# Weight units fetched two to a transfer, in runs of 8 KB a partition, on three double buffers

## The reference, cut to what matters

```python
def reference(x, ...):
    x = first_block(x, ...)    # S5 scan + banded attention + gates, w_out, then PEER
    return second_block(x, ...) # modulation by c, NSA attention + short conv, w_out, then PEER

def peer(xn, w_query, sub_keys, u_tab, v_tab):   # in both blocks; 8 heads, 16 experts a head
    q = xn @ w_query                             # (512, 1024)
    # scores against 2 x 128 sub keys a head, top 16 of each, top 16 of their 256 sums
    # -> 128 expert numbers and 128 gates for each token
    a = einsum('cd,ced->ce', xb, u_tab[eb])      # 128 rows of u for each token
    w = gb * gelu(a)
    return einsum('ce,ced->cd', w, v_tab[eb])    # 128 rows of v for each token
```

## Time and profile before

| | before |
|---|---|
| median of 3 runs | 3286.17 us (3284.38 to 3288.89) |
| the profiled execution's own time | 3282.93 us |
| its span in the trace | 3281.1 us |
| granted TensorE clock | 0.85 |
| bytes read from HBM | 1289.62 MB, 394 GB/s over the span |
| busy: TensorE, VectorE, ScalarE, GpSimd | 75%, 71%, 41%, 34% |

### The profile page before, as it was taken

One profiled execution on the slowest core, in us unless ns is written; L12 is line 12 of the kernel. 1 busy time (PEld: TensorE's weight loads), 2 busy tenths in 40 slices (PEclk: granted clock), 3 DMA queues, 4 the chain that ended last, 5 costly groups with the idle time before them and its releaser, 6 DMA issues.

```text
span 3281.1 us, 40578 instructions
## 1 busy us (share of the span) xinstructions
PE 2445.8 (75%) x14052; PEld 1029.2 (31%) x14052; DVE 2320.1 (71%) x5500; ACT 1330.7 (41%) x3602; POOL 1129.2 (34%) x1038
## 2 busy tenths in 40 slices
PE   8868779776797777979787869878887655554555
PEld 3442333223332233335342426423334211111111
DVE  7439694778839787385875685987866777777644
ACT  2114432444424444243583343467734433333322
POOL 0012342324413243243343333443433444443432
PEclk9979889987898988989888979878888877778777
DMA  9899999999999999999999999999999999999997
GB/s 247 304 351 415 399 410 386 411 397 414 413 389 416 415 411 412 371 397 401 383 379 388 397 402 399 406 419 410 378 411 400 413 420 420 419 418 409 420 420 318
DMA packets 214057, 1295.01 MB, mean 395 GB/s; under 512 B 26934, under 2 KB 30294, under 8 KB 82776
## 3 DMA queue, kind: packets, MB, share of 16 engines
q0 software_dynamic: 148320, 1076.50, 80.9%
q1 hardware_dynamic: 64860, 213.81, 17.2%
q10 hardware_dynamic: 672, 2.12, 0.2%
HBM read 1289.62 MB, written 2.71 MB: 394 GB/s over the span
## 4 chain that ended last, share of the span: by engine, by line
PE 35%; DMA 25%; DVE 22%; issue 8%; ACT 4%; POOL 3%; SPq 0%; POOLq 0%; DVEq 0%; ACTq 0%
PE ps L1722 12%; DMA ring<-in_k_uv,idx 10%; DMA ring<-in_k_vu,idx 9%; PE ps L1802 9%; DVE ring L415 9%; DMA wsl<-in_k_wu 6%; PE ps L2096 6%; POOL ring L2400 3%; DVE big L470 2%; PE ps L2106 2%; ACT L1249 2%; PE ps L1779 1%; PE ps L1977 1%; DMA wsl<-in_k_wmod 1%; ACT diag L1249 1%
## 5 line engine op out<-in xcount | busy, mean ns | idle before, releaser
L1722 PE MATMUL ps<-ring,diag 64*64 64x512 f32 x8192 | 1255.7, 738 | 483.1 <-ACT diag L1249 459.1
L415 DVE CUSTOM_DVE_ANT_0 ring<-ring,xn 128x1024 f32<-128x1024 f32 x1024 | 1238.8, 1220 | 440.9 <-DMA ring<-in_k_vu,idx 231.7
L2400 POOL DMA_INDIRECT ring<-in_k_vu,idx x514 | 559.5, 1089 | 1136.7 <-DVE aw L415 645.6
L2400 POOL DMA_INDIRECT ring<-in_k_uv,idx x510 | 563.6, 1105 | 940.1 <-DVE aw L415 643.2
L1722 PEld LDWEIGHTS ps<-ring,diag 64*64 64x64 f32 x8192 | 308.2, 157 | 1240.0 <-ACT diag L1249 733.2
L1249 ACT ACTIVATE aw<-aw 128x2 f32<-128x2 f32 x512 | 103.7, 202 | 1008.8 <-DVE aw L415 1007.3
L1802 PE MATMUL ps<-wsl,xT 128*128 128x512 f32 x896 | 427.6, 623 | 36.5 <-DMA wsl<-in_k_wu 32.3
L1249 ACT ACT_TABLE_LOAD x339 | 434.9, 1283 | 22.8 <-issue 10.7
L1249 ACT ACTIVATE diag<-gid,aw 128x64 f32<-128x64 f32 x1024 | 312.0, 342 | 315.1 <-PE ps L1722 298.9
L1249 ACT ACTIVATE gid<-ident,gate 128x64 f32<-128x64 f32 x1024 | 292.4, 332 | 0.0
L1802 PEld LDWEIGHTS ps<-wsl,xT 128*128 128x128 f32 x896 | 167.0, 196 | 296.0 <-issue 226.4
(11 more groups left out here) (264 smaller groups left out, 2112.1 us busy)
## 6 DMA issues: line engine op xcount, KB each, us to landing
wsl<-in_k_wu SPq DMA_DIRECT2D x342, 512.0 KB, 8.8
wsl<-in_k_wmod SPq DMA_DIRECT2D x40, 512.0 KB, 6.4
ring<-in_k_vu,idx POOLq DMA_INDIRECT x514
ring<-in_k_uv,idx POOLq DMA_INDIRECT x510
ring<-in_k_wmod SPq DMA_DIRECT2D x8, 512.0 KB, 10.5
wsl<-in_k_wu SPq DMA_DIRECT2D x8, 280.0 KB, 26.4
hres<-in_x SPq DMA_DIRECT2D x4, 512.0 KB, 6.0
pers<-L1d POOLq DMA_DIRECT2D x8, 256.0 KB, 13.0
```

Of the source, the lines that this page charges most:

```text
L415: V(v.tensor_tensor_reduce(u_row(s), u_row(s), xn[:, n % 3, :], 1.0, 0.0, ALU.mult, ALU.add, aw[:, b, k:k + 1]), ("dot", s))
L1722: r = t.matmul(PA[half][64 * q:64 * q + 64, :], diag[64 * half:64 * half + 64, s % (2 * PAIR), :], v_row(s)[64 * half:64 * half + 64, 512 ...
L2400: Q(p.indirect_dma_start(out=both_rows(s), out_offset=None, in_=tab, in_offset=bass.IndirectOffsetOnAxis(ap=idx[:, n % 2, k:k + 1], axis=0 ...
```

## The change

The list of units is turned into `order`, in which an empty place follows each unit of `sk`, so that every pair of places (0 and 1, 2 and 3, ...) is two units of the same matrix and tile, or `sk` and nothing. `two_units(k)` takes the place of `unit(k)`: it waits for the use of both units that were in the pair of buffers, and issues one transfer for both (1 MB; 512 KB for `sk`). The host lays the two units of a pair side by side for each partition, so that a partition's part is one run of 8 KB; in the units of 280 columns the SBUF side stays in pieces. The eight early units become four transfers in the same manner. What TensorE waits for and marks stays one unit at a time: both marks of a pair stand on the one transfer. `extra(k)` is called ahead of each pair; all its places are at the first unit of one. The products and their order are the same.

```diff
-        early = [carve(rflat, at + 1024 * e, 2, 512)[0] for at in (2048, 11264) for e in range(4)]
+        early2 = [carve(rflat, at + 2048 * e, 4, 512)[0] for at in (2048, 11264) for e in range(2)]
+        early = [w[:, 2 * e:2 * e + 2, :] for w in early2 for e in range(2)]
...
-        unit_at = {(n, name, b, u): k for k, (n, name, b, u, *_) in enumerate(units)}
+        order = [w for u in units for w in ([u, None] if u[1] == "sk" else [u])]
+        unit_at = {w[0:4]: k for k, w in enumerate(order) if w}
+        assert all(x[0:3] == y[0:3] for x, y in zip(order[0::2], order[1::2]) if y)
...
-            def unit(k):
-                n, name, b, u, nk, key, c0, nn, at = units[k]
-                if k >= NWS:
-                    Y.wait_ge("unit_used", k - NWS)
+            def two_units(k):
+                n, name, b, u, nk, key, c0, nn, at = order[k]
+                count = 2 if order[k + 1] else 1
+                for j in range(k, k + count):
+                    if j >= NWS and order[j - NWS]:
+                        Y.wait_ge("unit_used", j - NWS)
                 src = A["k_wmod" if name == "mod" else "k_wu%d" % (n // 4)]
-                src = src[at:at + 256 * nn].rearrange("(p k n) -> p k n", p=128, n=nn)
-                Q(s.dma_start(wsl[:, k % NWS, :, 0:nn], src), "w%d" % (k % NWS), ("unit", k))
+                src = src[at:at + 256 * nn * count].rearrange("(p k n) -> p k n", p=128, n=nn)
+                dst = wsl[:, k % NWS:k % NWS + count, :, :].rearrange("p j k n -> p (j k) n")[:, :, 0:nn]
+                Q(s.dma_start(dst, src), "w%d" % (k % NWS), *[("unit", k + j) for j in range(count)])
...
-                    for e, w in enumerate(early):
-                        src = A["k_wmod"][131072 * e:131072 * e + 131072].rearrange("(p k n) -> p k n", p=128, n=512)
-                        Q(s.dma_start(w, src), "early%d" % e, ("early", e))
+                    for e, w in enumerate(early2):
+                        src = A["k_wmod"][262144 * e:262144 * e + 262144].rearrange("(p k n) -> p k n", p=128, n=512)
+                        Q(s.dma_start(w, src), "early%d" % e, ("early", 2 * e), ("early", 2 * e + 1))
...
-            unit(0)
-            unit(1)
+            two_units(0)
             load(craw[:, :, :], A["k_s5c"], "craw")
-            for k in range(2, NWS):
-                unit(k)
+            for k in range(2, NWS, 2):
+                two_units(k)
...
-            for k in range(NWS, len(units)):
+            for k in range(NWS, len(order), 2):
                 extra(k)
-                unit(k)
+                two_units(k)
...
-        arr["k_wu%d" % layer] = np.concatenate(laid)
-    arr["k_wmod"] = I["w_mod_2"][0].reshape(4, 2, 128, 12, 512).transpose(3, 0, 2, 1, 4).reshape(-1)
+        both = [np.stack([x.reshape(128, -1) for x in laid[k:k + 2]], 1).reshape(-1) for k in range(0, len(laid), 2)]
+        arr["k_wu%d" % layer] = np.concatenate(both)
+    arr["k_wmod"] = I["w_mod_2"][0].reshape(2, 2, 2, 128, 12, 512).transpose(4, 0, 3, 1, 2, 5).reshape(-1)
```

More of the change, by code:

```diff
@@ L2426, in extra @@
             def extra(k):
-                n, name, b, u = units[k][0:4]
+                n, name, b, u = order[k][0:4]
                 if (n, name, b, u) == (0, "attb", 0, 0):
```

## The result

| | before | after |
|---|---|---|
| median | 3285.28 us (6 runs, 3276.84 to 3288.89) | 3298.41 us (6 runs, 3294.60 to 3301.26) |
| ratio | | 1.0049, 95% interval 1.0034 to 1.0064 |
| the profiled execution's own time, span | 3282.93, 3281.1 us | 3297.68, 3296.1 us |
| granted TensorE clock | 0.85 | 0.846 |

The change makes the kernel 0.5% slower, where 0.4% faster was forecast. The median lies 0.4 us over the top of the range, 3298 us. The ratio is formed over the runs and is not the quotient of the two medians, which is 1.0040.

The account below looks back on a forecast made before the run. It took DMA bytes to bound full stretches and a chain of TensorE and its partners the others. Terms -6.6, -7.5, +2 and zeros summed to -12.1 us: 3274 us against 3286.17, range 3248 to 3298.

Parts of the forecast that it names:

- Term 4: In branch, pairs issued when both buffers are used: a 9.3 us cover against 8.3 us landings, so 0.
- rival C: In branch and route, TensorE waits for pairs: slower, 3303 us, or 3294 in a milder form; chance 0.12.
- term 1: In full DMA stretches, 8 KB pieces make each weight unit 0.038 us cheaper: -6.6 us.
- Term 3: Where weight streams start or end on an empty buffer, both units must land: +2 us, bounds 0 and +21.
- term 2: In win, weights get half the queue turns; gathers move to branch, where DMA has room: -7.5 us, bounds 0 and -21.6.
- A: The turn gives back all the room in branch: 3258 us, down to 3248; chance 0.16.
- B: Only order moves; gathers missing after win are fetched in full stretches: 3283 us; chance 0.24.
- D: SP's queue cuts 8 KB pieces in two, leaving only the costs of pairing: 3288 us; chance 0.03.
- E: Where weights run alone, in the first 240 us, fewer transfers save fixed cost: 3264 us; chance 0.03.

Follow-up runs that it names:

- two4: Against the kernel before: pairs issued only when both buffers are used, but as two transfers of 4 KB pieces; ratio 1.0045.
- branch_two: Against the kernel before: only in branch, route and their like, pairs issued when both buffers are free, as two transfers of 4 KB pieces; ratio 1.0035.
- one4: Against the kernel before: pairs issued when both buffers are used, as one transfer of 4 KB pieces, 280-column pairs as two transfers; ratio 1.0125.
- b7: The kernel before with seven buffers of one unit in place of six; ratio 0.9982, 3279.02 against 3281.95 us.
- after7: The changed kernel with seven buffers, a pair that would go round the end fetched as two units; ratio to the kernel before 1.0009.
- after_mv: The changed kernel with the L2d loads ahead of tile pair 4's third weight block issued one pair later; ratio to the kernel before 1.0062.

## Why the prediction was wrong

**Term 4 is the step that failed: "I take 0; the cover is these 9.3 us".** Measured: two4 +0.45% (15 us), branch_two +0.35%. And the rows it rested on said so. The earlier trace rows has both paces: two units in 3.65 us, but also four in 7.06 us, with one slot of 1.02 us behind either. The cover was taken from the slow pace, 4.67 us a pair; at the quick one a pair goes in 3.5 to 4 us, and two pairs are 7 to 8 us, less than the 8.3 us in which a unit landed at the median. The maximum of 10.8 us stood beside it. The cover of the slow pace and the median delay were compared, where each of 16 pairs in a row has its own. The chain shown above is one of them: 8.48 us to land, and TensorE out of units. This is rival C's mechanism at C's place, with a chance of 0.12. Its price was about right in the milder form: 3 x 16 x 0.3 = 14 us, and branch_two, the late issue in these places and their like alone, costs 0.35%, 11.5 us. That 3298.4 lies between C's 3294 and 3303 us is luck beside that: C took the full gain of term 1 off, and knew nothing of what landing as a whole and `win` cost.

**Term 3, "+2 us", was too small as well.** Under the old turns landing as a whole costs 0.80% (one4 against two4), 26 us, over ten times the charge; the upper bound was 21. A stream at DMA's pace was said to lose the second unit's move once. The traces show that it lost far more: over the span TensorE's products stood 101 us for units in one4 and 73 in two4 (60 in the kernel before), 28 us more, of which 10 lie before 240 us and 16 between 240 and 1400. Which starts of which streams carry them, no run took apart. The 33 waits and 30.9 us on which the bound rests count weight loads and products together; the products alone had 15 waits, 10.6 us. In the `w_mod` stretch 130:240 of the changed kernel the same sum of both rose from 30.9 us to

```profile
  DMA wsl<-in_k_wmod: 52.3, 26
```

and still the product of slot 8 was not later than before: there the waits moved. In all, the products of the changed kernel stood 57 us for units, against 60 and 63 in the two traces of before: 32 us before 240 us, where it was 11 and 18, and 13 us from 240 to 1400, where it was 45 and 35. The waits that went were those of `win`, where TensorE, as term 2 shows below, then stood for ScalarE instead.

**Term 1 was right in its price.** Queues of 1060:1100, after:

```profile
q0 software_dynamic: 1389, 10.09, 61.0%
q1 hardware_dynamic: 907, 6.64, 40.0%
```

6.64 MB in 40.0% of 40 us are 0.415 MB a us, where it was 0.401. The 564 and 550 us above are 14 us of engine time less, against 384 x 0.038 = 15 for the 192 pairs. It bought nothing that can be seen in the time, since idle time grew by more. Two counts beside it were off: 196 transfers are saved and not 199, since a unit of `sk` has no partner, and the packets under 8 KB fell by 52,288, twice the 25,000 given, because both halves of a piece leave that class; it is the sum of all packets that fell by 27,712.

**Term 2 was right about the turn and wrong about its fruit.** In 240:300, after:

```profile
q0 software_dynamic: 1745, 12.72, 51.2%
q1 hardware_dynamic: 1707, 12.40, 49.9%
```

Nearly equal bytes, where the kernel before has 14.52 and 10.34 MB. (In 1060:1100 they are not equal, 10.09 and 6.64: the six buffers fill and q1 falls silent, as term 2 said itself.) The Trainium skill (DMA: Bandwidth & Descriptors, Queues, rings and completion order) has each engine go round the queues by packets, and the trace agrees. TensorE's waits for units in 1060:1100 went from 16.7 us to none, a unit or pair landed after

```profile
DMA to landing us min/median/max: 8.9/9.9/10.8
```

in place of 21.0 us. But the room in `branch` was to be used by it, -7.5 us; its rate went down instead, 393 to 367, because TensorE's chain got longer there: of the 6.4 us lost from slot 192 to 240, 2.8 are waits of its products for units and 2.8 are longer busy time. And in `win` of tile 3 the turn costs. In 1060:1100 VectorE's busy time fell from 37.98 to 34.69 us; it waited 3.5 us for gathers, where before it waited for none: three dots start at 1075.91, 1080.90 and 1085.89, 5.0 us apart, the gathers' pace at half of the turns. Its top-16 work stands behind the dots in its order. The top-16 work of a head ended 8.4 us later, the first line before and the second after:

```profile
1113.13 0.15 DVE L908 RECIPROCAL rowB<-rowB 128x1 f32<-128x1 f32 x1
1121.52 0.15 DVE L911 RECIPROCAL rowB<-rowB 128x1 f32<-128x1 f32 x1
```

ScalarE has the head's exponentials ahead of emptying TensorE's banks (`big <- ps`), and so TensorE, which had all its units, stood for that. Before:

```profile
1113.79 1.09 PE L1722 MATMUL ps<-ring,diag 64*64 64x512 f32 x8 [2.25 <-ACT big L1249]
1115.86 5.40 PE L1802 MATMUL ps<-wsl,xT 128*128 128x512 f32 x8
```

and after:

```profile
1122.19 1.98 PE L1725 MATMUL ps<-ring,diag 64*64 64x512 f32 x8 [11.53 <-ACT big L1252]
1126.10 6.19 PE L1805 MATMUL ps<-wsl,xT 128*128 128x512 f32 x8
```

The pause cost more than itself. The granted clock was 0.50, the lower of TensorE's two levels (1.2 and 2.4 GHz), from 1115 to 1130, behind a pause of 11.5 us; before it was 0.89 over these 15 us. Eight products that take 3.70 us at the full clock took 6.19. From the end of slot 248 to that of 256 the idle time of the products grew from 11.3 to 16.6 us and their busy time from 29.5 to 32.7, together the step of 8.5 us. In the other four kernels with 8 KB pieces in that `win` it is the same: 11.5 us of wait for ScalarE, no wait for units, 32.7 us busy. And the rate in 1100:1160 fell to 373 GB/s. That is what "wrong" would look like by the prediction: `win` longer, VectorE waiting for gathers, the rate below 416. No run tested the late heads alone. b7, with 4 KB pieces, has 7.7 us of the wait for ScalarE and 5.1 us of the step, so units that come early may be enough.

**The sum.** As ratios: late issue +0.45%, landing as a whole +0.80%, 8 KB pieces (turn and cheaper bytes) -0.76%, together +0.49%. The forecast had 0, +2 us and -14 us. The third came out larger than forecast; the first two were taken as margins and are the result. The three are steps of one path, from before over two4 and one4 to the changed kernel, each known to 0.2 or 0.3 points; in another order they could be of other sizes.

**The rivals.** A is out (no room in `branch` was used). B, 0.24, would have been 3283 us and is out as well; after7, 1.0009, comes nearest to it, with a buffer more. D is out by the packet count. E: the first 240 us run at 296 GB/s in place of 298, so no gain from fewer transfers shows there. The 2 us of fixed cost behind E stand in the Trainium skill, DMA: Bandwidth & Descriptors, under Anatomy of one DMA, for transfers issued by GpSimd, and not under Measured, where the prediction places them. The Trainium skill, same page, Rules for kernel authors, asks for at least 1 MiB a DMA for most bandwidth. This case gains nothing by it: with weight transfers of 1 MB the rate over the span is 393 GB/s, with 512 KB 395.

## What to carry to other kernels

Joining two transfers into one is a change of buffering first and of bandwidth second. Count how many pieces of work stand ready when the refill is issued, take the user's quickest pace and the transfer's slowest landing from the trace, and compare these, not the middle ones; where the user is the engine that sets the pace, every shortfall counts in full. Before going to larger transfers, try one buffer more or less as it is: here 0.89% for one less showed how thin the cover was. When a view adds the waits of weight loads and of products, read the two apart. And profile the kernel before twice: a step of 5 to 8 us that five kernels seemed to share was a lucky spot in the first trace.

## What had not been expected of the hardware

- One transfer of 1 MB in 4 KB pieces is far worse beside gathers in 8 KB pieces than two of 512 KB (1.0125 against 1.0045), while the same 1 MB in 8 KB pieces is not (1.0049). The size of the contiguous piece moves a queue's share beside another queue: with 4 KB the weights had 42% of the bytes in 240:300 and 34% in 1060:1100, with 8 KB 49% and 40%. The time to land moves with it: in 1060:1100 a unit of 512 KB took 21.0 us with 4 KB pieces, a pair of 1 MB 9.9 us with 8 KB.
- SP can stand before a plain issue: the eight loads from L2d took 5.1 us to issue in one execution and 13.5 us in another of the same kernel. Why is not shown. The time did not follow it: after_mv, with 5.2 us, has the step from slot 368 to 376 as the others have.
- TensorE's clock hardly differs over the span, 0.85 granted before, 0.846 after and 0.841 to 0.851 in the other traces, and still it has a part where it matters: in the five kernels that lose 8 us from slot 248 to 256, some 3.2 us of it are longer busy time of the products, at a clock of 0.50 behind a pause of 11.5 us in the changed kernel's trace.
